# Attention of a hybrid decoder block, rebuilt feature-major: 512-column q, k and gate projections, scores over stacked high and low halves, values projected ahead

## The reference

```
q, k = rope(at_q), rope(at_k)
for window, dilation in ((128, 1), (512, 4), (2048, 16)):      # causal, 128 keys back in steps of the dilation
    o_i, lse_i = dilated_window_attention(q, k, v, window, dilation)
o_at  = sum(softmax(lse) * o) * silu(at_z)
mixed = concat([o_hg, o_at])
out   = rms_norm(x + mixed @ w_out) * final_norm_w
```

## Time and profile before

| what | value |
|---|---|
| runs shown | 1489.21 us median of 3 (1482.77 to 1491.72) |
| span of the profiled execution | 1485.4 us, 3.8 below the median |
| PE busy | 1398.0 us (94%) x10728 matmul records |
| weight loads (overlap PE) | 1266.5 us (85%) |
| DVE, ACT, POOL busy | 794.7, 494.6, 313.0 us |
| DMA | 104.95 MB, mean 71 GB/s |
| attention, 584 to 1281 us | 697 us, PE busy 649.26 |

### The profile page before, as it was taken

How to read it: one execution, slowest core, us unless ns; L and a number is a source line. 1 busy time by engine, 2 the same in 40 slices (tenths; PEclk the granted TensorE clock), 3 DMA queues, 4 the chain that set the end, 5 groups by cost and what they waited for, 6 DMA issues and landing times. The chain is left out here.

```text
span 1485.4 us, 31108 instructions
## 1 busy us (share of the span) xinstructions
PE 1398.0 (94%) x10728; PEld 1266.5 (85%) x10728; DVE 794.7 (53%) x2265; ACT 494.6 (33%) x1578; POOL 313.0 (21%) x437
## 2 busy tenths in 40 slices
PE   5999989999999999999899998999989998899997
PEld 5989989988897999877798777987789775799997
DVE  5846846774783876465444654455544554322222
ACT  5622221121122122445324453245531556311111
POOL 5733333243243233000010000100111003100000
PEclk9999999999999999999999999999999999999999
DMA  6420230122023012211130111301113012533331
GB/s 212 143 75 23 72 104 19 34 82 78 22 75 94 19 47 91 64 30 52 41 108 6 34 47 43 108 3 50 42 41 101 9 56 81 178 118 131 125 111 57
DMA packets 101910, 104.95 MB, mean 71 GB/s; under 512 B 17024, under 2 KB 82816, under 8 KB 101760
## 3 DMA queue, kind: packets, MB, share of 16 engines
q1 hardware_dynamic: 101760, 102.93, 22.0%
HBM read 69.21 MB, written 33.69 MB: 69 GB/s over the span
## 5 line engine op out<-in xcount | busy, mean ns | idle before, releaser
L522 PE MATMUL bank<-w_hi,u_hi 128*128 128x256 f32 x1792 | 532.3, 297 | 13.9 <-DVEq L1271 6.2
L524 PE MATMUL bank<-w_hi,u_lo 128*128 128x256 f32 x1792 | 509.7, 284 | 0.0
L523 PE MATMUL bank<-w_lo,u_hi 128*128 128x256 f32 x1792 | 509.3, 284 | 0.0
L522 PEld LDWEIGHTS bank<-w_hi,u_hi 128*128 128x128 f32 x1792 | 345.4, 193 | 68.2 <-issue 49.1
L523 PEld LDWEIGHTS bank<-w_lo,u_hi 128*128 128x128 f32 x1792 | 346.0, 193 | 0.2
L524 PEld LDWEIGHTS bank<-w_hi,u_lo 128*128 128x128 f32 x1792 | 345.2, 193 | 0.0
L1060 DVE TENSOR_TENSOR room<-room 128x256 f32<-128x256 f32 (+7 forms) x658 | 209.6, 360 | 60.3 <-POOL room L999 36.5
L1060 DVE TENSOR_TENSOR room<-bank,room 128x128 f32<-128x128 f32 (+1 forms) x336 | 110.3, 379 | 233.6 <-PE bank L524 186.2
L1295 DVE CUSTOM_DVE_ANT_0 room<-bank,room 128x256 f32<-128x256 f32 (+3 forms) x256 | 109.5, 449 | 161.8 <-PE bank L701 154.8
L937 POOL TENSOR_TENSOR w_lo<-stage,w_hi 128x512 fp32r<-128x512 f32 x72 | 95.0, 1323 | 449.2 <-ACT w_hi L774 449.1
L873 ACT ACTIVATE room<-room 128x256 f32<-128x256 f32 (+3 forms) x256 | 134.5, 530 | 14.1 <-DVE room L1295 11.9
(11 more groups left out here) (122 smaller groups left out, 2050.1 us busy)
## 6 DMA issues: line engine op xcount, KB each, us to landing
stage<-in_w_groups SPq DMA_DIRECT2D x80, 256.0 KB, 3.6
room<-in_x SPq DMA_DIRECT2D x32, 512.0 KB, 5.4
values_gates<-vg_tile SPq DMA_DIRECT2D x128, 128.0 KB, 1.7
room<-values_gates SPq DMA_DIRECT2D x48, 256.0 KB, 3.9
room<-values_gates SPq DMA_DIRECT2D x16, 512.0 KB, 4.3
mixed<-room SPq DMA_DIRECT2D x32, 256.0 KB, 2.3
room<-mixed SPq DMA_DIRECT2D x16, 512.0 KB, 4.7
out<-room SPq DMA_DIRECT2D x16, 512.0 KB, 2.9
```

Of the source, the lines that this page charges most:

```text
L522: nc.tensor.matmul(dst, lhs_hi(k), rhs_hi(k), start=(k == 0), stop=False)
L523: nc.tensor.matmul(dst, lhs_hi(k), rhs_lo(k), start=False, stop=False)
L524: last = nc.tensor.matmul(dst, lhs_lo(k), rhs_hi(k), start=False, stop=(k == KT_N - 1))
```

## The change

Prologue and HGRN units stay (the last HGRN unit is written out instead of looped, and computes the values of attention units 0 and 1 in place of values and gates of unit 0). Attention becomes 16 blocks (unit v, block b) of 4 tiles, written out without a loop:

- q, k and gate are projected feature-major, 512 tokens wide: groups A and B (first and second rotation half of q and k of both heads, 128 columns each) and Z (gate), each in `PARTS` = 4 parts of 6 matmuls of 512 columns. Three parts are filler in each tile; A and B of block n+1 and Z of block n fall in block n. There is no filler left after the first slot of tile 60 of 64.
- the values of units 2 and 3 are one dense pass of 16 tiles ahead of attention.
- DVE rotates q and k feature-major, ACT and DVE split them into halves, and 24 DMAs of 32 rows by 2 KB per block (`gather_keys`, `gather_queries`) put them into `ks[h]` (rows: high 1, high 2, low 1, low 2) and into two tiles per head `qd` (high over high, low over low). A score is then two float32r matmuls over 128 rows.
- values are loaded tile by tile (`load_near`, `load_far`). The mixing weights are spread over features by 8 transposes per block (`spread_weights`); DVE and POOL combine, and the gate is `0.5 z (1 + tanh(z/2))`. The result stays feature-major in DRAM, so that only the HGRN half of `mixed` needs transposes in the output stage (4, not 8), and the output projection is 48 matmuls of 512 columns per tile.
- the 8 pieces of the output weights (512 KB each) are loaded in tile 60 by ACT's queue and split in tiles 61 to 64.

```diff
+def filler_parts():
+    groups = []
+    for n in range(AT_BLOCKS):
+        if n + 1 < AT_BLOCKS:
+            groups += [("A", n + 1), ("B", n + 1)]
+        groups.append(("Z", n))
+    return [(kind, n, part) for kind, n in groups for part in range(PARTS)]
...
 # SP
+            def load_far(T):
+                v, t = divmod(T, TILES)
+                for kk in range(t // CH + 1):
+                    z = far_slot(T, kk) % FAR_SLOTS
+                    src = v_dram[v // 2, kk * BT:(kk + 1) * BT, (v % 2) * P:(v % 2 + 1) * P]
+                    sp.dma_start(far_v[:, z, :], src.rearrange("(m c) n -> c m n", c=CH)[T % CH]).then_inc(fv_landed[z], 16)
+            def gather_keys(n):
+                cols = slice((n % BLOCKS) * BT, (n % BLOCKS + 1) * BT)
+                for h in range(2):
+                    rows = slice(64 + 32 * h, 96 + 32 * h)
+                    for z, part in enumerate((hi1, hi2, lo1, lo2)):
+                        sp.dma_start(ks[h][32 * z:32 * z + 32, cols].bitcast(F32), part[rows, :].bitcast(F32)).then_inc(ks_landed, 16)
+            def gather_queries(n, h):
+                rows = slice(32 * h, 32 * h + 32)
+                for z, part in enumerate((hi1, hi2, lo1, lo2)):
+                    dst = qd[(4 * n + 2 * h + z // 2) % Q_SLOTS]
+                    for twice in range(2):
+                        at_row = 64 * twice + 32 * (z % 2)
+                        sp.dma_start(dst[at_row:at_row + 32, :].bitcast(F32), part[rows, :].bitcast(F32)).then_inc(qd_landed[h], 16)
...
+            for T in range(AT_TILES):
+                if i == 3:
+                    if n + 1 < AT_BLOCKS:
+                        after(s_ready, 3 * T + 3)
+                        gather_queries(n + 1, 1)
+                        if g == 3:
+                            gather_keys(n + 1)
...
+                    after(e_done, 4 * T + 4)
+                    sp.dma_start(stat_dram[n]..., st_far[n % 2]...).then_inc(stat_stored, 16)
+                if i == 0 and n >= 1:
+                    after(stat_stored, 16 * n)
...
+                if i == 2:
+                    if n >= 1:
+                        after(comb_done, n)
+                        store_output(n - 1)
+                    if n + 1 < AT_BLOCKS:
+                        after(qk_lo, n + 2)
+                        if n >= 1:
+                            after(s_ready, 12 * n)
+                        gather_queries(n + 1, 0)
+                        if g != 3:
+                            gather_keys(n + 1)
+                    if n + 2 < AT_BLOCKS:
+                        after(b_read, n + 2)
+                        load_table(n + 2)
...
+                if T >= 1:
+                    after(pv_mm, T)
+                    load_far(T)
+                    if T + 1 < AT_TILES:
+                        load_near(T + 1)
...
 # PE
+            pe.wait_ge(out_done0, HG_UNITS * 2 + ONE)
+            pe.wait_ge(out_done1, HG_UNITS * 2 + ONE)
+            for kind in "AB":
+                for part in range(PARTS):
+                    filler(kind, 0, part)
+            for t in range(TILES):
+                phase1_tile(DENSE + 1, t, "dense")
+            for kind, n, part in fill[0:AHEAD]:
+                filler(kind, n, part)
...
+            for T in range(AT_TILES):
+                scores(T)                 # near: 2 x 2 matmuls of 256; far: 2 x 2 of 128(g+1); j == 0 waits for the gathers
+                filler                    # 6 matmuls of 512
+                if T % CH == 1 and T > CH:
+                    spread_weights(T // CH - 1)
+                    filler
+                turn_near_far0(T - 1)
+                if not (T % CH == 1 and T > CH): filler
+                turn_far1(T - 1)          # shares bank 4 with the near transposes: waits until ACT copied them
+                filler
+                weigh(T - 1)
...
 # ACT, tile T
+                take_near(T - 1); exps(T, 0)
+                if i == 2: queries_keys_hi(n + 1)     # two copies of 512
+                take_far1(T - 1); exps(T, 1); take_output(T - 1)
+                if i == 0: exp_differences(n - 1)
...
 # DVE, tile T
+                if i == 1:
+                    mix_weights(n - 1)
+                    weigh_outputs(n - 1)
+                lows(T, 0); take_far0(T - 1)
+                if i == 0: rope_a(n + 1)              # 2 passes of 512
+                if i == 2: queries_keys_lo(n + 1)     # 2 passes of 512
+                lows(T, 1)
+                if i == 1: rope_b(n + 1)              # 6 passes of 512
+                if i == 0: differences(n - 1)
```

More of the change, by code:

```diff
@@ L81, in blocks_before @@
     return sum(k == kind for k, _ in HG_STEPS[:HG_STEPS.index(("T", tile))])
[L84 to L131, removed]
@@ new lines, in filler_bank, with far_slot, build @@
+def filler_bank(kind, n):
+    if n == 0 and kind != "Z":
+        return 0 if kind == "A" else 7
+    index = 3 * n + {"A": -1, "B": 0, "Z": 4}[kind]
+    return 7 if index % 2 else 0
+def far_slot(tile, kk):
+    n = tile // CH
+    full, g = n // BLOCKS, n % BLOCKS
+    return full * CH * 10 + CH * (g * (g + 1) // 2) + (tile % CH) * (g + 1) + kk
+def build(nc, x, w_groups, w_units, w_out, norm_w, gate_g, lb_logits, final_w, rope, near_mask, far_mask, tri_masks, out):
+    vg_dram = nc.dram_tensor("values_gates", (HG_UNITS, SEQ, GC), F32, kind="Internal").ap()
+    v_dram = nc.dram_tensor("values", (2, SEQ, GC), F32, kind="Internal").ap()
+    mixed_dram = nc.dram_tensor("mixed", (SEQ, D // 2), F32, kind="Internal").ap()
+    at_dram = nc.dram_tensor("attended", (D // 2, SEQ), F32, kind="Internal").ap()
+    stat_dram = nc.dram_tensor("far_stats", (AT_BLOCKS, BT * 4), F32, kind="Internal").ap()
@@ L226, in build @@
[L226 to L238, removed]
@@ new lines, in build, with take @@
+        near_m = at("near_m", SG, [2 * P])
+        o_nf = at("o_nf", VG, [2, BT])
+        spot = [VG + 2 * BT]
+        def take(name, shape, dt=F32):
+            where = spot[0]
+            spot[0] += int(np.prod(shape))
+            assert spot[0] <= NW, spot[0]
+            return at(name, where, shape, dt), where
+        ks = [take(f"ks{h}", [SEQ], F32R)[0] for h in range(2)]
+        qd = [take(f"qd{s}", [BT], F32R)[0] for s in range(Q_SLOTS)]
+        t1, t1_at = take("t1", [BT])
+        t2, t2_at = take("t2", [BT])
@@ new lines, in spread_weights @@
+            def spread_weights(n):
+                pe.wait_ge(wts_ready, n + 1)
+                for f, w in enumerate((r1, t3)):
+                    if f == 0:
+                        pe.wait_ge(pt_near_far1, 8 * (n + 1))
+                    else:
+                        pe.wait_ge(pt_far0, 4 * (n + 1))
+                    for j in range(CH):
+                        last = nc.tensor.transpose(bank[4 + f][:, j * P:(j + 1) * P], w[:, j * P:(j + 1) * P], ident[:, :])
+                    last.then_inc(wt_mm, 1)
@@ L1024, in _ @@
-            with pool.Fori(0, AT_UNITS - 1) as v:
-                attention(v, True)
-            attention(AT_UNITS - 1, False)
-            pool.wait_ge(comb_stored, AT_UNITS * 64 + ONE)
-            nc.gpsimd.memset(o_half, -0.5).then_inc(pool_step, 1)
+            with pool.Fori(0, HG_UNITS - 1) as u:
+                hg_unit(u)
+            hg_unit(HG_UNITS - 1)
+            for i in range(4):
+                split_lo(2 * DENSE + 2, i, 0)
+            split_unit_lo(HG_PIECES)
+            split_unit_lo(HG_PIECES + 1)
```

1167 lines of the change are left out of this document (653 added, 514 removed).

## The result

The changed kernel takes 1622.49 us (median of 4 runs, 1618.66 to 1627.10) against 1489.34 (4 runs, 1482.77 to 1491.72): ratio 1.0907, 95% interval 1.0881 to 1.0933. It is slower by 9%; I had forecast 1475, with 1525 as the upper end.

What follows compares the result with a forecast made beforehand. Attention was to be bound by q and k's path through SP's queue, not PE. Tile 0 at 654.2, fifteen blocks 572.3, clock 15, 41 from tile 60, output stage gaining 15.8: span 1471.3, median 1475; range 1400 to 1525.

Steps and rivals of the forecast that it cites:

- the price of a gather: SP's queue, 24 gathers a block: 0.38 us per issue, the last landing 1.7 us after its issue.
- The path up to there: Block's waits and DVE, ACT work before the gathers: low halves ready 23.7 us into a block at g = 0, 24.6 at g = 1.
- the clock: PE in attention: waits of 3 us lower its granted clock, costing 1.0 us per block, 15 in all, at most about 1.7.
- start: Ahead of attention: HGRN's last result, first projections, 4.8 of idle and the dense pass put tile 0 at 654.2.
- 15 blocks, up to head 1's first score of tile 60: Attention: blocks of 35.5 to 40.9 us, 572.3 for fifteen, and 15 for the clock: tile 60 at 1241.5.
- tail: From tile 60 to the first output matmul: 41 us; output-weight loads add nothing, or up to 15 if late.
- PE's content: PE in attention: scores 0.96 to 1.39 us a tile, blocks of 28.4, 30.4, 33.4, 36.4 us for g = 0 to 3.
- everything hides: Rival, attention: the q and k path hides and PE's content sets the blocks; 1366 us, chance 0.10.
- A slower queue: Rival, SP's queue: a gather costs 0.47 us or more; 1507, or 1518 with a slower clock; chance 0.25 together with slower scores.
- a shorter path: Rival, attention: waits in i1, 1.7 per block, vanish as DVE and ACT run ahead; 1435 us, chance 0.20.
- Scores at four times the price: Rival, PE's float32r scores: up to 3 us more per tile at g = 3; 1520 or more, nearly excluded.
- Tanh: ACT in i3: priced at nothing; otherwise two table loads of 1.28 us per block, 38 us of ACT.

Runs made afterwards that it cites:

- the bare program: Not this kernel: a program issuing only groups of 12 DMAs, each group alone; SBUF to SBUF took 0.63 us an issue on SP.
- three queues: Changed kernel with keys' gathers on POOL's queue, low queries on ACT's, high queries on SP's ahead of the low halves: 1507.97 us.
- Six bulk DMAs: Changed kernel without stacking: 6 DMAs of 128 rows carry the bytes of 24 gathers, scores of other data: 1443.99 us.
- three queues, ends: Against three queues: first block's gathers behind the stores of the values, part on ACT, output stage's loads one tile later: 1506.47 us.
- the best version: Changed kernel with 20 gathers a block on three queues, low-by-low product left out, lower rows of low queries zeroed: 1479.19 us, 0.9947 of the kernel before.

## Why the prediction was wrong, step by step

**The mechanism was right**: attention's pace is set by the path of q and k through SP's queue, not by PE, and the waits fall at the far values and at the next first score, as said.

**The step that failed is the price of a gather**: "A gather has 32 rows; no row shows one. Its bounds are 0.33 and 0.49; I take 0.38, near the lower, because of the fewer rows". It is 0.63. The bounds came from DMAs out of DRAM, and a gather goes from SBUF to SBUF. That fewer rows are cheaper is true out of DRAM (0.45 for 0.55), not here: between two places in SBUF the bare program shows no dependence on rows or bytes. In the block above the last landing was 3.05, not 1.7. Together 24 x 0.25 + 1.35 = 7.4 us. The chain shows it: from the low halves to the score of head 1 it takes 898.65 - 879.32 = 19.3 us, where I had 11.8. That landing was a long one, behind an issue that took 1.6 (the four low gathers 3.54 for the usual 2.49); the median is 2.0. Over all 15 blocks the stretch from the low halves to the score of head 1 is 104 us longer than in my working, 7.0 a block, and 24 x 0.25 = 6.0 of that are the gathers' issues.

**The path up to there was right from i1 on.** From the first score of i1 to the low halves it was 16.8 in the working for g = 0 and 16.6 in the trace (862.75 to 879.32); over 15 blocks it is 3 us shorter than in the working. The first tile of a block was not right: in the same block it lasts from 850.89 to 862.75, 11.9 us for my 6.9. It follows the waits, and its first matmuls of 512 columns start 0.43 apart, where they are 0.23 from 858 on. Over 15 blocks the first tiles are 27 us longer, against the 15 that I had set aside for the clock.

Against my span of 1471.3 the sum of the measured parts is then:
- start: tile 0 at 667.3, not 654.2, +13.1. 10.5 is PE waiting for `vg_tile`, since block 0's gathers stand between the stores of the values in SP's queue. That queue was costed for blocks 1 to 15 only. Moving those gathers (on three queues) gave 7 at once and nothing in the end.
- 15 blocks, up to head 1's first score of tile 60 at 1367.6 (head 0's is at 1364.2): 700.3, not 587.3, +113.0, 7.5 a block. It is made of the three stretches above: 104 + 27 - 3, less the 15 for the clock. Six bulk DMAs on SP take it all away and more.
- clock: in the four blocks from 865.66 on PE was busy for 145.9 us at 0.85 to 0.90, in the same four of the run with six bulk DMAs (842.04 to 986.45) 137.1 at 0.95 to 1.00. That is 2.2 us a block for my 1.0 (my bound was 1.7). It lies inside the stretches above and isn't additive to them.
- tail: 62.0 from tile 60 to the first output matmul, not 41, +21. With six bulk DMAs the tail from block 14's spread weights to block 15's in the output stage is 58.7 for 59.8 after, so gathers have next to no part in it. The chain that ended last shows four things in the tail: 3.9 us in which ACT issues the loads of output weights ahead of its exponentials, 5.8 in which SP issues nine loads of the output stage ahead of the store of block 14, that store's landing, 8.0 for a median of 3.1, and 4.8 of ACT's splits of the output weights:

```profile
1377.33 0.42 ACTq L1054
...
1399.04 0.65 SPq L409
1399.73 8.00 DMA attended<-gate
...
1420.08 2.84 ACT wo_hi L1020 x3
```

  With 4.9 for what the landing is above its median these are 19.4 of the 21. That is read from the chain and not shown by a run: issuing SP's loads one tile later (three queues, ends) made the tail only 2.5 shorter. I had named the 4 MB of weights as a risk of 15 and priced it at nothing.
- rest, behind the first output matmul: 3.5, not followed up. The output tiles are 11.37 apart, 11.4 as said. 13.1 + 113.0 + 21 + 3.5 = 150.6 = 1621.9 - 1471.3.

**PE's content** was short as well, which one queue hides. I priced the scores at 0.96 to 1.39 us a tile; they take 0.59 + 1.05 = 1.64 at g = 3, and in the four blocks of the run with six bulk DMAs PE was busy for 137.1 us instead of my 128.6. A part is that the far scores load every fourth column as weights, 0.24 us a load, which no row of the kernel before could tell: at g = 0 four of them take 0.93 where I had 4 x 0.12, at g = 3 1.05 for 4 x 0.227. So "everything hides" is not 1366; six bulk DMAs, which still leave some waits, show 1444.

**The rivals.** A slower queue is what happened, and it was priced at 1507 to 1518 with a gather at 0.47: the right rival with a wrong bound, so that even its far end missed by 100 us. With 0.63 its own formula (15 x 24 x 0.25 = 90) gives 1565; with the whole 104 of that stretch, the start and the tail it is 1613. Everything hides, a shorter path: not seen. Scores at four times the price: no, far scores of 512 columns start 0.26 apart (1.05 / 4).

**Tanh** costs what I said, nothing: three table loads in the whole trace, the last at 664.79, ahead of tile 0. By the Trainium skill (ScalarE: Activation LUTs, Table sets: the hidden batching unit) exp and tanh share a set; the trace agrees, with 16 gates of 0.595 us and no load beside them. The other rule of the Trainium skill that I weighed, that starting a DMA is usually small beside the DMA (DMA: Bandwidth & Descriptors, Issuing engines are not separate DMA queues), holds for one gather, 0.63 against 2.0, and is the wrong picture for 24 in a queue: 15.1 us of issues and one landing. The measurement decides.

## What to carry to other kernels

Count the DMAs that one queue issues between a result and its first reader, multiply by an issue of the same kind (source and destination memory) and add one landing; if the trace has no issue of that kind, bound it by more than its nearest relatives or measure it in a bare program of twelve. Test a suspected queue by adding useless tiny DMAs and by merging the real ones: a slope equal to the issue's price both ways settles it. A long wait behind a crowded queue need not be a loss of its own: here reordering the one queue only renamed it.

## What was not expected of the hardware

- An issue from SBUF to SBUF costs 0.63 us on SP or ACT, on SP whatever the rows and bytes (4 to 128 KB), and 0.50 on POOL. From DRAM it is 0.45 (32 rows) or 0.55 (128), from SBUF to DRAM 0.45 or 0.48.
- SP's and ACT's queues issue beside each other at nearly full pace. With POOL's as a third SP took 0.96 us an issue, and 64 KB landed in 3.5 to 3.7 us on ACT and POOL, for 2.0 on ACT before.
- PE pays about 0.15 to 0.17 us for each change between 128-row and 64-row matmuls; 102 us in this kernel (1681.06 for 1579.04).
- Matmuls whose weights are every fourth column start 0.24 us apart at 128, 256 and 512 columns; with plain weights it is 0.12, 0.20 and 0.22 (float32r).

Open: why an issue between two places in SBUF is dearer than one with DRAM at either end, what three queues share, and what holds the best version at 1479 when six bulk DMAs reach 1444.
